# A first query projection taken by blocks of 512 columns, with the first head's selection and the first four gathers placed under its later blocks

## What is computed

```python
def peer_block(x, wq, k1, k2, U, V):
    qq = (x @ wq).reshape(N, PEER_H, 2, PEER_DQ // 2)      # 2048 x 2048 weights, 8 heads
    s1 = jnp.einsum('nhd,hkd->nhk', qq[:, :, 0], k1)       # 128 keys per half
    s2 = jnp.einsum('nhd,hkd->nhk', qq[:, :, 1], k2)
    v1, i1 = lax.top_k(s1, 16)
    v2, i2 = lax.top_k(s2, 16)
    cand = (v1[..., :, None] + v2[..., None, :]).reshape(N, 8, 256)
    sc, ci = lax.top_k(cand, 16)
    e = i1[ci // 16] * 128 + i2[ci % 16]                   # expert numbers
    g = jax.nn.softmax(sc, axis=-1)
    act = gelu(einsum('nd,nhjd->nhj', x, U[e]))
    return einsum('nhj,nhjd->nd', g * act, V[e])
```

## Time and profile before

| what | value |
|---|---|
| median of 3 runs | 2510.61 us (2499.58 to 2512.24) |
| profiled execution, time | 2507.47 us |
| profiled execution, span | 2505.7 us |
| TensorE busy (matmuls) | 2154.6 us, 86% |
| VectorE busy | 1516.5 us, 61% |
| ScalarE busy | 458.8 us, 18% |
| GpSimd busy | 377.3 us, 15% |
| bytes moved by gathers | 671.11 MB |
| bytes moved by the hardware queue | 173.45 MB |

### The profile page before, as it was taken

The page is one execution under the profiler, slowest core; times in us unless marked ns, Lnnn a source line. Parts: engine busy times, 40 slices in busy tenths (PEclk is TensorE's granted clock), DMA queues, the critical chain, the costliest instruction groups (busy, mean ns, idle before and its releaser), DMA issues.

```text
span 2505.7 us, 20801 instructions
## 1 busy us (share of the span) xinstructions
PE 2154.6 (86%) x7662; PEld 1204.6 (48%) x7662; DVE 1516.5 (61%) x2686; ACT 458.8 (18%) x880; POOL 377.3 (15%) x363
## 2 busy tenths in 40 slices
PE   6999999987888999989999988777777877877776
PEld 5999999855575343434444443322232322222221
DVE  4434543485485666675444568888888755555555
ACT  3323332324363001121000112111111100100001
POOL 0000000100000212111121212212222222222221
PEclk9999999999899999999999999999999999999999
DMA  6544444323987999999999999999999999999997
GB/s 185 163 134 135 135 145 154 117 91 97 340 351 300 423 425 379 422 386 426 425 417 423 399 428 409 417 414 412 409 405 411 415 428 429 428 429 428 427 429 314
DMA packets 155534, 845.89 MB, mean 338 GB/s; under 512 B 9350, under 2 KB 97218, under 8 KB 108762
## 3 DMA queue, kind: packets, MB, share of 16 engines
q0 software_dynamic: 46080, 671.11, 63.5%
q1 hardware_dynamic: 109354, 173.45, 20.0%
HBM read 834.31 MB, written 10.21 MB: 337 GB/s over the span
## 4 chain that ended last, share of the span: by engine, by line
PE 53%; DMA 32%; DVE 9%; issue 4%; ACT 1%; SPq 0%; POOL 0%; DVEq 0%; POOLq 0%
DMA rows_in<-in_peer_uv,expert 30%; PE bank L277 20%; PE bank L359 7%; PE bank L1180 6%; PE bank L1181 6%; PE bank L1182 6%; DVE rows_in L662 3%; PE bank L1158 1%; DVE diag L636 1%; PE bank L324 1%; DMA wf<-in_w_out 1%; PE bank L326 1%; PE bank L325 1%; PE bank L1260 1%; PE bank L1349 1%
## 5 line engine op out<-in xcount | busy, mean ns | idle before, releaser
L277 PE MATMUL bank<-rows_in,diag 128*128 128x512 f32 (+1 forms) x2560 | 1190.7, 612 | 262.4 <-DVE diag L636 262.2
L662 DVE CUSTOM_DVE_ANT_0 rows_in<-rows_in,x2n 128x2048 f32<-128x2048 f32 x320 | 733.6, 2292 | 532.2 <-DMA rows_in<-in_peer_uv,expert 531.9
L277 PEld LDWEIGHTS bank<-rows_in,diag 128*128 128x128 f32 (+1 forms) x2560 | 452.9, 183 | 982.4 <-issue 545.4
L567 POOL DMA_INDIRECT rows_in<-in_peer_uv,expert x320 | 365.7, 1143 | 1455.2 <-PE bank L277 1306.2
L449 ACT ACTIVATE dots<-dots 128x1 f32<-128x1 f32 x320 | 65.0, 203 | 1515.3 <-DVE dots L662 1515.3
L1180 PE MATMUL bank<-xnh,wh 128*128 128x336 f32 (+2 forms) x928 | 295.3, 318 | 4.7 <-DVE wl L1606 4.7
L1181 PE MATMUL bank<-xnl,wh 128*128 128x336 f32 (+2 forms) x928 | 291.6, 314 | 0.0
L1182 PE MATMUL bank<-xnh,wl 128*128 128x336 f32 (+2 forms) x928 | 291.5, 314 | 0.0
L1606 DVE TENSOR_TENSOR wl<-wring,wh 128x2048 fp32r<-128x2048 f32 (+1 forms) x58 | 132.1, 2279 | 211.4 <-ACT wh L1413 211.4
L1180 PEld LDWEIGHTS bank<-xnh,wh 128*128 128x128 f32 (+1 forms) x928 | 174.9, 188 | 12.4 <-issue 11.1
L1181 PEld LDWEIGHTS bank<-xnl,wh 128*128 128x128 f32 (+1 forms) x928 | 175.0, 189 | 1.3
(11 more groups left out here) (303 smaller groups left out, 1381.5 us busy)
## 6 DMA issues: line engine op xcount, KB each, us to landing
wring<-in_w_in SPq DMA_DIRECT2D x28, 2048.0 KB, 8.3
wf<-in_w_out SPq DMA_DIRECT2D x16, 1024.0 KB, 8.8
wf<-in_peer_wq SPq DMA_DIRECT2D x16, 1024.0 KB, 6.5
wk<-in_w_out SPq DMA_DIRECT2D x32, 512.0 KB, 11.2
wk<-in_peer_wq SPq DMA_DIRECT2D x32, 512.0 KB, 10.4
kT<-in_keys_t SPq DMA_DIRECT2D x16, 512.0 KB, 5.8
vpage<-in_cache_v SPq DMA_DIRECT2D x16, 512.0 KB, 6.2
rows_in<-in_peer_uv,expert POOLq DMA_INDIRECT x320, 12.5
```

What stands on the lines that cost most here:

```text
L277: mm = pe.matmul(accs[t][d][0:w, :], diag[r % ND][:, 0:w], rows_in[r % NG][:, D + 512 * d:D + 512 * d + 512], start=False, stop=(j == ROUN ...
L567: nc.gpsimd.indirect_dma_start(out=rows_in[r % NG][:], out_offset=None, in_=UV_DR, in_offset=bass.IndirectOffsetOnAxis(ap=ids[:, j:j + 1], ...
L662: nc.vector.tensor_tensor_reduce(u, u, x2n[t][:], 1.0, 0.0, ALU.mult, ALU.add, dots[t % 2][:, j:j + 1]).then_inc(S["dot_done"], 1)
```

## The change

The query projection of tile 0 is now cut the other way. A load n = 16 to 31 holds 512 rows of `peer_wq` by 512 columns, as four pieces side by side in a slot; four such loads (KU = 4) make one block of 512 columns, and blocks are done one after the other. A bank closes after each block, and the two query steps of a block stand inside the next one. The selection of head 0 is spread over the remainders of n = 23, 24 and 25, and GpSimd no longer waits for the end of the projection: gathers 0 and 1 wait for the expert numbers of head 0 alone, gathers 2 and 3 also until load 23 is used. To make room for the four `rows_in` slots, loads 24 to 31 have three slots in place of six, and `wfh` has three in place of four from n = 16 on. The keys are loaded ahead of the projection's weights in place of in their middle.

```diff
+KU = 4
+FEW = KC + 8
+    def slot_of(n):
+        return n % NF if n < FEW else n % (NF // 2)
+    def high_slot(n):
+        return n % NH if n < KC else n % (NH - 1)
+        def column_blocks():
+            for n in range(KC, 2 * KC):
+                d, k = (n - KC) // KU, (n - KC) % KU
+                slot_ready(n)
+                src = a["peer_wq"][0][KU * P * k:KU * P * (k + 1), 512 * d:512 * d + 512].rearrange("(k p) c -> p k c", p=P)
+                sp.dma_start(wf[slot_of(n)][:].rearrange("p (k c) -> p k c", k=KU), src).then_inc(wf_in[slot_of(n)], 16)
...
-        full_rows(a["peer_wq"][0], 1, range(KC // 2))
         sp.dma_start(kT12[:], ...).then_inc(S["keys_in"], 16)
-        full_rows(a["peer_wq"][0], 1, range(KC // 2, KC))
+        column_blocks()
         take(sp, ("wq", 0, 3))
...
+        def first_queries(outs):
+            def unit(n):
+                d, first = (n - KC) // KU, (n - KC) % KU * KU
+                pe.wait_ge(S["wk_lo"], n + 1)
+                for i in range(KU):
+                    k = first + i
+                    ...three matmuls of 512 columns into outs[d]
+            for d in range(4):
+                n = KC + KU * d
+                unit(n)
+                if d:
+                    query(0, d - 1, "qt")
+                unit(n + 1)
+                if d == 1:
+                    pe.wait_ge(S["keys_in"], 16)
+                if d:
+                    query(0, d - 1, "pS")
+                for k in range(2, KU):
+                    unit(n + k)
+            query(0, 3, "qt")
+            query(0, 3, "pS")
...
     def weight_high(act, n):
-        if n >= NH:
-            full_read(act, n - NH)
+        earlier = [k for k in range(n) if high_slot(k) == high_slot(n)]
+        if earlier:
+            full_read(act, earlier[-1])
...
-                for n in range(KC + 2, 2 * KC):
+                for n in range(KC + 2, KC + 6):
                     weight_high(act, n)
+                for d in range(4):
+                    evacuate(("wq", 0, d), qqn[0][:, 512 * d:512 * d + 512])
+                    later = range(KC + KU * d + 6, min(KC + KU * d + 10, 2 * KC))
+                    for n in later[0:1]:
+                        weight_high(act, n)
+                    evacuate(("qt", 0, d), x2T[0][:, 4 * d:4 * d + 4, :])
+                    for n in later[1:2]:
+                        weight_high(act, n)
+                    evacuate(("pS", 0, d), sc[0][:, 4 * d:4 * d + 4, :])
+                    for n in later[2:]:
+                        weight_high(act, n)
...
     def tail_pool(pool):
-        take(pool, ("wq", 0, 3))
+                if r == NG // 2:
+                    full_read(pool, FEW - 1)
...
                 for n in range(KC + 5, 2 * KC):
                     weight_low(dve, n)
+                    for u in range(HSTEPS)[2 * (n - KC - 7):2 * (n - KC - 6)] if n >= KC + 7 else ():
+                        head_step(0, 0, u)
...
         dve.wait_ge(S["x2n_done"], 4)
-        for u in range(HSTEPS):
-            head_step(0, 0, u)
+        gate_share(0, 0)
```

More of the change, by code:

```diff
@@ L192, in rounds_by, with slot_use, slot_ready, full_rows @@
         return min(point, POINTS_B) * 3 // 2 + max(0, point - POINTS_B)
-    def full_read(eng, n):
-        part, k = n // KC, n % KC
-        if k == KC - 1:
-            take(eng, (("wo", "wq")[part], 0, 3))
-        else:
-            eng.wait_ge(S["wk_used"], (KC - 1) * part + k + 1)
+    def slot_of(n):
+        return n % NF if n < FEW else n % (NF // 2)
+    def high_slot(n):
+        return n % NH if n < KC else n % (NH - 1)
+    def slot_use(n):
+        return sum(1 for k in range(n) if slot_of(k) == slot_of(n))
+    def full_read(eng, n):
+        if n == KC - 1:
+            take(eng, ("wo", 0, 3))
+        elif n < KC:
+            eng.wait_ge(S["wk_used"], n + 1)
+        elif n % KU == KU - 1:
+            take(eng, ("wq", 0, (n - KC) // KU))
+        else:
+            eng.wait_ge(S["wk_used"], KC - 1 + (n - KC) // KU * (KU - 1) + n % KU + 1)
+    FULL_USED = KC - 1 + KC // KU * (KU - 1)
     def tail_sync(sp, out):
[L204 to L210, removed]
+        def slot_ready(n):
+            before = [k for k in range(n) if slot_of(k) == slot_of(n)]
+            if before:
+                full_read(sp, before[-1])
+        def full_rows(rows_):
+            for n in rows_:
+                slot_ready(n)
+                sp.dma_start(wf[slot_of(n)][:], a["w_out"][0][P * n:P * n + P, :]).then_inc(wf_in[slot_of(n)], 16)
+        def column_blocks():
+            for n in range(KC, 2 * KC):
+                d, k = (n - KC) // KU, (n - KC) % KU
+                slot_ready(n)
+                src = a["peer_wq"][0][KU * P * k:KU * P * (k + 1), 512 * d:512 * d + 512].rearrange("(k p) c -> p k c", p=P)
+                sp.dma_start(wf[slot_of(n)][:].rearrange("p (k c) -> p k c", k=KU), src).then_inc(wf_in[slot_of(n)], 16)
         def weight_rows(w, part):
@@ L231, in tail_sync @@
         sp.wait_ge(S["iqz_done"], 1)
-        full_rows(a["w_out"][0], 0, range(3))
+        full_rows(range(3))
         xp, xs = a["x_prompt"][0], a["x_sample"].rearrange("b t d -> (b t) d")
@@ L299, in query @@
             close(mm)
[L301 to L309, removed]
+        def first_queries(outs):
[4 more added lines that the diff above has]
+                    k = first + i
+                    if d == 0:
+                        evacuated(pe, ("xt", 0, k // 4))
+                    cols = slice(512 * i, 512 * i + 512)
+                    pe.matmul(outs[d][:], lh[:, k, :], wfh[high_slot(n)][:, cols], start=(k == 0), stop=False)
+                    pe.matmul(outs[d][:], ll[:, k, :], wfh[high_slot(n)][:, cols], start=False, stop=False)
+                    mm = pe.matmul(outs[d][:], lh[:, k, :], wfl[slot_of(n)][:, cols], start=False, stop=(k == KC - 1))
+                if k == KC - 1:
+                    close(mm)
+                else:
+                    mm.then_inc(S["wk_used"], 1)
+            for d in range(4):
[12 more added lines that the diff above has]
+            query(0, 3, "pS")
         def product(part, lhs, beside):
@@ L332, in product @@
                 for k in range(KC - 4):
-                    if part and k % 4 == 0:
-                        evacuated(pe, ("xt", 0, k // 4))
                     for d in range(4):
                         cell(k, d)
-                    if k == 0 and part == 0:
+                    if k == 0:
                         sample_turn()
[L339 to L350, removed]
+                for half in ((0, 1), (2, 3)):
+                    for k in range(KC - 4, KC):
+                        for d in half:
+                            cell(k, d)
                 return
@@ L383, in project @@
             if g == 0:
-                product(1, (), first_query)
-                for q, what in ((1, "pS"), (2, "qt"), (3, "qt"), (2, "pS"), (3, "pS")):
-                    query(0, q, what)
+                product(1, (), beside)
                 return
```

54 lines of the change are left out of this document (26 added, 28 removed).

## The result

| | before | after |
|---|---|---|
| median | 2512.17 us (11 runs, 2499.58 to 2523.81) | 2533.43 us (11 runs, 2523.39 to 2541.5) |
| profiled execution, time | 2507.47 us | 2533.43 us |
| profiled execution, span | 2505.7 us | 2531.2 us |

The ratio estimated from all runs is 1.0098, with a 95% interval of 1.0081 to 1.0114: 24.6 us slower. The medians differ by 21.3 us and the two profiled executions by 26.0, so a difference of a few us between single executions says little. The busy times of the engines hardly moved (TensorE 2152.9 us, VectorE 1516.6, ScalarE 457.9, GpSimd 374.8), so the time went into waits.

The account below looks back on a forecast made before the run. It took the query projection's close to bound the kernel, ahead of a tail with DMA engines and TensorE full. Profiled 2507.5 + 28.6 (later TensorE start) - 6 (row waits) = 2530.1, said as 2531 us; range 2508 to 2544.

Parts of the forecast that it names:

- The close: End of tile 0's query projection: forecast at 811 us instead of 781.4.
- load 29: Query projection load issued at 774.8 us beside four gathers: 512 turns against their 512 pieces, so it ends with them.
- The product: Tile 0's query projection on TensorE: its close was forecast 29.6 us late.
- What stands behind the last landing: After load 31 lands, at 803 us: rounding, remainder, 2.7 us on TensorE and 1 for a slowed clock.
- Slots and selection: Projection without gather contention: three load slots and head 0's steps among VectorE's remainders put the close 12.2 us late.
- rival 1: Projection loads don't suffer from the gathers: close at 793.6 us, 12.2 late, total 2513; chance 0.16.
- The gathers: Under the projection: 8.4 MB of gathers share the DMA engines with 3.7 MB of loads, all landed by about 802.
- The gathers' issue beside remainders: Slower gather issue on GpSimd beside VectorE's remainders 26 and 27: priced at nothing, 2 to 3 us at the upper end.
- The gap behind the close: From the close to TensorE's first `wk`: 1 us shorter, since that load no longer meets gathers.
- Given back: TensorE's 26 blocks from 804.8 to 900.1 us: 6 us of waits for gathered rows go.
- The total: Whole kernel: 2530.1 us summed against the profiled execution, which stood 3 us under the median; so 2531.
- Rival 2: Behind 795 us: the 8.4 MB of transfers moved forward come back in full, 19.8 us less; chance 0.11.

Follow-up runs that it names:

- late_gathers: The changed kernel, but GpSimd's gathers wait again for the end of tile 0's query projection; 2535.72 us, ratio 1.0115 to the kernel before.
- late_gathers_hold: late_gathers, but GpSimd also waits until the first half load `wk` of tiles 1 and 2 has landed; 2522.56 us, ratio 1.0063 to the kernel before.
- whole_rows: The changed kernel, but each query projection load fetches 128 rows in 8 KB pieces instead of 512 pieces of 2 KB; one run, 2528.09 us.
- late_both: late_gathers, with the selection of head 0 also put back behind all remainders; ratio 1.0050 to the kernel before.
- six_slots: The changed kernel with six slots for all loads; gathers 0 and 1 stay early, 2 and 3 wait for the projection's end; ratio 1.0045 to the kernel before.
- columns_only: late_both with six slots again for all loads; ratio 1.0008 to the kernel before.
- early_two: six_slots, gathers 2 and 3 held until the second `wk` landed, six `wk` issued before the inputs, VectorE's input wait later; ratio 1.0006 to the kernel before.

## Why the prediction was right, and where it was not

It said 2531 us, and 2533.43 was measured. The mechanism is the one it named: the loads issued beside the gathers take turns with them piece by piece. The close, forecast at 811, came at 810.9; load 29, forecast to end with the gathers, took 23.9 us; VectorE waited for `wfh` and ScalarE for `wf` between 776 and 797; TensorE's first `wk`, forecast near 824, came at 824.7, and TensorE did not wait for a row in the 75 us after. The mechanism is shown by late_gathers (15.4 us of the product go with the gathers), late_gathers_hold and whole_rows. That so many times agree to a us is in part luck, as the points below show.

Point by point:

- **The product.** It grew by 32.6 us, not 29.6. The close agreed to 0.1 us only because TensorE began the product at 731.1 in this trace and not at 734.2. That is luck.
- **What stands behind the last landing.** The sum let load 31 land at 803 and put 7.9 us behind it. It landed at 800.2, and the close came 10.7 us later. The chain runs by load 29 and not by 31: with the remainder of 29 ready at 799.3, TensorE took loads 29, 30 and 31 and one set of scores in 11.6 us without a wait. Load 29 alone took 5.0 us in place of 2.7, at a granted clock of 0.53. The sum had 1 us for that, though the row that it cites has 2.9 (9.8 against 6.9). An error of 3 us too late and one of 3 us too little cancel here.
- **Slots and selection.** The prediction's rival 1 holds the product without contention, 12.2 us longer. late_gathers has it 17.1 us longer (1.3 + 7.0 + 8.8). This is the term that was mis-sized. The loads that nothing hides are the two that it named, 28 and 31, and their landings (4.99 and 4.88 us) were well priced at 4.8. What was not is TensorE's use of them, 2.7 us each in the sum and 4.6 in the trace; that is 3.8 of the 4.9 us, and about 3 of them are the lower clock (3.1 each in late_both). The prediction had no clock term in this case.
- **The gathers** were then worth 17.4 us in the prediction (29.6 - 12.2) and 15.4 in the runs. The last landing is set by the 12.1 MB from the gathers' first data on, forecast 802 to 803, measured about 800. So the two errors partly cancel: whatever comes sooner waits for the same transfers.
- **The gathers' issue beside remainders**, priced at nothing. It took 2.90 and 1.73 us in place of 1.11 and 0.94. They lay beside two remainders of VectorE, from 765.5 to 770.0. The Trainium skill ("SBUF — State Buffer", section "SBUF: two separate sides") lets a VectorE operation with two inputs in SBUF hold the shared ports for the whole instruction against a GpSimd operation that reads SBUF. The longer issues fit that, for a gather reads its expert numbers from SBUF. The prediction's reading of it, that the gathers would start only behind both remainders, does not fit: the issue of gather 0 had ended at 768.8, while the second remainder ran. The remainders kept their 2.29 us. It cost nothing that shows: gather 0 went out 4.5 us sooner than forecast (765.9 against 770.4), 3 of them because TensorE began the product sooner.
- **The gap behind the close**, forecast 1 us shorter with no gather in it. It has the same 13.8 us, and the first `wk` the same 11.38. The gathers of before had met nothing of it that counted; the wait is that of the 3.7 MB.
- **Given back**, forecast 6 us. This came out as forecast: TensorE did the 26 blocks of the earlier trace rows in 89.3 us in place of 95.2, as the two rows below show. Another 1.1 us came from the first two loads `wk` (8.7 us in place of 9.8). TensorE was 22.5 us late behind these blocks, 22.2 at 1099, and 25.5 at the end. The forecast for the end was 22.6, so what is left of its error in these two executions lies behind 1100 us, where it had said that nothing changes. Why 3.3 us went there no run shows, and it is less than the scatter between executions.

```profile
833.27 3.60 PE L303 MATMUL bank<-h,c 128*128 128x512 f32 x8
...
922.53 7.03 PE L307 MATMUL bank<-rows_in,diag 128*128 128x512 f32 x16
```

- **Rival 1**, "the loads don't suffer from the gathers, 2513", fell: load 29 took 23.9 us and not 5 to 8. With the product of late_gathers its own sum would have given some 5 us more. late_gathers is not this rival's kernel, since its gathers stand beside the loads behind the close, which costs 2535.72 us. I left that out of what I expected of late_gathers and six_slots.
- **The total.** The sum, 2530.1, stood against the profiled execution, 3 us under the median of before; with all 3 added it would have said 2533 and not 2531.
- **Rival 2**, that the 8.4 MB moved forward come back, fell: from 824 to 930 us the DMA share is 0.92 at 375 GB/s. The transfers do not bound this stretch, since TensorE is full there and only four slots hold rows.

What stays open is the size of what comes back. Row 0's use relative to the first product goes with the time, but not one to one: +34.1 us there are +28.8 in late_gathers, +31.5 are +24.6 in the change, +10.6 are +12.5 in late_both, +6.9 are +2.0 in columns_only, and -4.2 are +1.5 in early_two. No run follows the rows past 900 us one by one, and the differences of columns_only and early_two are within their intervals.

## What to carry to other kernels

A transfer that is moved into an idle stretch is not free when a load that something waits for is issued beside it: list the loads that will be in flight, count their pieces, and count on one piece of the gathers going with each of their pieces. Ask of each early start how many buffers it fills; with four slots the lead is four rows, and behind them the engine that uses the rows sets the pace. Work that seems to be hidden in a gap may hold something off that would do harm in it: the selection of head 0 kept the gathers away from the loads of that gap.

## What the runs showed of the hardware

- Gathers and the hardware queue share the DMA engines by pieces and not by bytes. Beside gathers of 16 KB pieces, a load of 1 MB in 2 KB pieces took 23.9 us (after), loads of 1 MB in 8 KB pieces came 7.4 us apart (whole_rows), and loads `wk` of 512 KB in 4 KB pieces 6.2 us apart (late_gathers, 825.8 and 832.0).
- Four gathers, the first issued 0.3 us after the first of 3.7 MB of loads, put the last of these off from 11.4 to 28.2 us after its issue (late_gathers). With the first issued 8.9 us after it they put it off by nothing that shows (before).
- A gather's issue on GpSimd took 2.90 and 1.73 us beside a VectorE operation with two inputs, and 1.11 (the first) and 0.94 us otherwise (after, before).
- TensorE used one load of 1 MB (twelve matmuls of 512 columns) in 3.1 us at a granted clock of 1.00 and in 4.6 at 0.64 (late_both, late_gathers).
